# Column sets of the gated feed-forward units: one group later, with sums carried between PSUM banks by ScalarE copies

## What is computed

```python
def swiglu(x, w_gate, w_up, w_down):
    return (jax.nn.silu(x @ w_gate) * (x @ w_up)) @ w_down

for layer in range(DEPTH):            # first stack; the second has the same shape
    mix = even_mixer(hn, ...) if layer % 2 == 0 else odd_mixer(hn, ...)
    x = x + rms_norm(mix, norm_mix_post[layer])
    hn = rms_norm(x, norm_ffn_pre[layer])
    x = x + rms_norm(swiglu(hn, ...), norm_ffn_post[layer])

# in odd_mixer, per channel, the decay rate that a gate scales:
log_a = -RG_C * gate_r * jax.nn.softplus(-lam)
```

## Time and profile before

| what | value |
|---|---|
| median of 3 runs | 1228.73 us (1228.41 to 1228.79) |
| profiled execution | 1228.27 us, of which the span of its instructions 1226.4 us |
| TensorE (PE) busy | 1219.6 us, 99% |
| VectorE (DVE) busy | 1013.4 us, 83% |
| ScalarE (ACT) busy | 751.4 us, 61% |
| GpSimd (POOL) busy | 97.9 us, 8% |
| granted TensorE clock | 1.00 of full in the whole span |
| DMA, mean share of 16 engines | 4 to 6 tenths in most slices |

### The profile page before, as it was taken

One profiled execution on the slowest core, in us unless ns is written; L12 is line 12 of the kernel. 1 busy time (PEld: TensorE's weight loads), 2 busy tenths in 40 slices (PEclk: granted clock), 3 DMA queues, 4 the chain that ended last, 5 costly groups with the idle time before them and its releaser, 6 DMA issues.

```text
span 1226.4 us, 16404 instructions
## 1 busy us (share of the span) xinstructions
PE 1219.6 (99%) x6284; PEld 1013.5 (83%) x6284; DVE 1013.4 (83%) x1436; ACT 751.4 (61%) x1154; POOL 97.9 (8%) x123
## 2 busy tenths in 40 slices
PE   9999999999999999999999999999999999999998
PEld 7778888888888888888888888888888888888887
DVE  8986999889788798878887756988888785989787
ACT  8875756555998655555687536465556643745552
POOL 2520000000100100000232000000001300000000
PEclk9999999999999999999999999999999999999999
DMA  8544455546654564645555234556455315464552
GB/s 342 154 142 138 173 207 187 206 172 206 205 195 169 187 206 172 237 174 206 198 187 172 69 104 145 203 178 230 172 206 190 133 35 206 173 211 166 206 189 86
DMA packets 32830, 218.75 MB, mean 178 GB/s; under 512 B 3936, under 2 KB 4576, under 8 KB 7408
## 3 DMA queue, kind: packets, MB, share of 16 engines
q1 hardware_dynamic: 30384, 210.32, 48.8%
q0 software_dynamic: 1648, 6.88, 2.2%
q10 hardware_dynamic: 720, 0.50, 0.1%
HBM read 216.64 MB, written 1.05 MB: 177 GB/s over the span
## 4 chain that ended last, share of the span: by engine, by line
PE 94%; DVE 4%; issue 1%; ACT 1%; DMA 0%; SPq 0%; DVEq 0%; ACTq 0%
PE PS L521 26%; PE PS L523 26%; PE PS L522 26%; PE PS L527 6%; PE PS L1022 2%; PE PS L1046 1%; PE PS L558 1%; PE PS L630 1%; PE PS L624 1%; PE PS L625 1%; PE PS L556 1%; PE PS L555 1%; DVE WL L2050 1%; DMA RAW<-in_w 0%; PE PS L963 0%
## 5 line engine op out<-in xcount | busy, mean ns | idle before, releaser
L2050 DVE TENSOR_TENSOR WL<-RAW,WH 128x2048 fp32r<-128x2048 f32 (+3 forms) x198 | 420.8, 2131 | 97.8 <-ACT WH L1364 97.8
L1364 ACT ACTIVATE WH<-RAW 128x2048 fp32r<-128x2048 f32 (+3 forms) x200 | 356.6, 1789 | 119.2 <-PE PS L523 119.1
L521 PE MATMUL PS<-WH,HTh 128*128 128x512 f32 (+1 forms) x752 | 296.9, 395 | 0.1
L523 PE MATMUL PS<-WH,HTl 128*128 128x512 f32 (+1 forms) x752 | 291.6, 388 | 0.0
L522 PE MATMUL PS<-WL,HTh 128*128 128x512 f32 (+1 forms) x752 | 291.3, 387 | 0.0
L523 PEld LDWEIGHTS PS<-WH,HTl 128*128 128x128 f32 x752 | 141.2, 188 | 29.4
L521 PEld LDWEIGHTS PS<-WH,HTh 128*128 128x128 f32 x752 | 141.3, 188 | 29.3 <-DVE WL L2050 1.1
L522 PEld LDWEIGHTS PS<-WL,HTh 128*128 128x128 f32 x752 | 141.4, 188 | 26.9
L521 PE MATMUL PS<-WH,YAh 128*128 128x512 f32 x354 | 139.9, 395 | 0.1
L523 PE MATMUL PS<-WH,YAl 128*128 128x512 f32 x354 | 138.0, 390 | 0.0
L522 PE MATMUL PS<-WL,YAh 128*128 128x512 f32 x354 | 137.8, 389 | 0.0
(11 more groups left out here) (546 smaller groups left out, 2051.0 us busy)
## 6 DMA issues: line engine op xcount, KB each, us to landing
RAW<-in_w SPq DMA_DIRECT2D x196, 1024.0 KB, 4.9
WL<-in_w POOLq DMA_DIRECT2D x2, 1024.0 KB, 9.0
BC<-in_rows POOLq DMA_DIRECT2D x4, 512.0 KB, 4.1
YG<-in_mem POOLq DMA_DIRECT2D x4, 512.0 KB, 4.9
X<-in_x SPq DMA_DIRECT2D x2, 512.0 KB, 5.4
RAW<-in_w SPq DMA_DIRECT2D x4, 256.0 KB, 5.7
BC<-in_s SPq DMA_DIRECT2D x1, 512.0 KB, 11.3
YG<-in_s SPq DMA_DIRECT2D x1, 512.0 KB, 9.2
```

The lines of the kernel that those rows point to most:

```text
L521: e.matmul(out, ah, bh, start=start, stop=False, skip_group_check=joined)
L523: return e.matmul(out, al, bh, start=False, stop=stop, skip_group_check=joined)
L1364: e.activation(WH[:, c % NW, w], RAW[:, c % NR, w], ACT.Copy).then_inc(S.hi, 1)
L2050: e.tensor_tensor(WL[:, c % NW, w], RAW[:, c % NR, w], WH[:, c % NW, w].bitcast(f32), SUB).then_inc(S.lo, 1)
```

## The change

**Order of groups.** `SETS` becomes (3, 6), and each bank of a group and of a turned tile gets a new place (`BANKS`, `FOLD_BANK`). Turned tiles no longer have banks 4 and 5 for themselves.

**The set.** Of the four chunks of a set, the first two now carry 2 x 7 block products, and the last two are plain: again 90 matmuls. The sums stay in four banks in all, C11, C21, C12 and C22. After the first 6 matmuls ScalarE copies C11 to C22 (`cu`); after 12 it copies C12 into SBUF (`c7`); VectorE adds C22 and that copy into C21 (`j1`) after 24; ScalarE copies C22 to C12 (`cv`), and VectorE adds once more into C22 (`j2`). So two VectorE additions and three ScalarE copies stand where eight and one stood. TensorE waits for `cu`, `j1`, `cv` and `j2` within the set.

**Weight sums.** Per block row two sums are made ahead (`set_ahead`, `set_hi`) and two inside the set (`late_raw`, `late_hi`), rounded into the unused first quarter of `WH`/`WL` of the same chunk and two blocks of `YBh`/`YBl`. `RAW` of the two chunks is held until the late sums are made. The first plain chunk of the set is split in two halves of 2 x 512 (`half_of`, `half_rest`), the first of which has a semaphore of its own.

**Fold places.** Two tiles are turned at a time, between the two chunks of a group; groups 9 and 10 are turned inside `wide_mm`.

**Decay rates** move to the recurrent mixer, between its convolutions and splits.

```diff
-SETS = (2, 6)
+SETS = (3, 6)
+FOLD_BANK = (0, 6, 7, 0, 1, 6, 2, 3, 0, 6, 4)
 # TensorE
             def set_mm(f, a, cs, folds):
...
+                add(C11, Y(0, 0, 0), W(0, 1), start=True)
+                rests_ready(e, cs[1])
+                add(C11, Y(1, 0, 0), W(1, 1), stop=True).then_inc(S.qa, 1)
...
+                add(C12, sum_of(0, 2), T(0, 0, 1), start=True).then_inc(S.qt, 1)
+                add(C12, sum_of(1, 2), T(1, 0, 3), stop=True).then_inc(S.qt, 1)
+                e.wait_ge(S.cu, n + 1)
+                add(C22, sum_of(0, 1), T(0, 1, 2)).then_inc(S.qt, 1)
+                add(C22, sum_of(1, 1), T(1, 1, 4)).then_inc(S.qt, 1)
+                add(C11, Y(0, 1, 0), W(0, 2))
+                add(C11, Y(1, 1, 0), W(1, 2))
+                e.wait_ge(S.j1, n + 1)
+                add(C22, sum_of(0, 0), T(0, 0, 5))
+                add(C22, sum_of(1, 0), T(1, 0, 6)).then_inc(S.qc, 1)
+                e.wait_ge(S.n1l, n + 1)
+                for t, b in enumerate((C11, C21)):
+                    for k in (4, 5):
+                        rows(cs[2], k, t, 0, b)
+                e.wait_ge(S.cv, n + 1)
...
-                group(1)
-                fold(0)
-                set_mm(f, 2, cs[4:8], lambda: fold(1))
-                group(4)
-                fold(2)
-                fold(3)
-                group(5)
+                group(1)
+                group(2, lambda: two_folds(0))
+                set_mm(f, 3, cs[6:10], lambda: fold(2))
+                group(5, lambda: two_folds(3))
                 set_mm(f, 6, cs[12:16], lambda: fold(5))
-                group(8)
-                fold(6)
-                fold(7)
-                group(9)
-                fold(8)
+                group(8, lambda: two_folds(6))
+                group(9, lambda: fold(8))
                 group(10)
-                fold(9)
-                wide_mm(cs[22:], ..., lambda: fold(10), 1, f)
+                wide_mm(cs[22:], ..., lambda: two_folds(9), 1, f)
 # ScalarE
+                def column_set(a, *folds):
+                    half_of(cs[2 * a - 1], 0)
+                    e.wait_ge(S.qa, n + 1)
+                    copy(PS[:, C22, :], PS[:, C11, :]).then_inc(S.cu, 1)
+                    half_of(cs[2 * a - 1], 1)
+                    e.wait_ge(S.qt, 4 * n + 2)
+                    copy(FB[f][5][:, 3, :], PS[:, C12, :]).then_inc(S.c7, 1)
+                    late_hi(a, 0, 0)
+                    late_hi(a, 1, 0)
+                    tanh(a - 1)
+                    e.wait_ge(S.qc, n + 1)
+                    copy(PS[:, C12, :], PS[:, C22, :]).then_inc(S.cv, 1)
...
 # VectorE
+                def column_set(a, *folds):
+                    late_raw(a, 0, 0)
+                    late_raw(a, 0, 1)
+                    late_raw(a, 1, 0)
+                    half_rest(cs[2 * a - 1], 0)
+                    set_rest(a, 5, 0, 0)
+                    e.wait_ge(S.c7, n + 1)
+                    e.wait_ge(S.qt, 4 * n + 4)
+                    e.tensor_tensor(PS[:, C21, :], PS[:, C22, :], M7, ADD).then_inc(S.j1, 1)
...
+            decay_rates(2)
+            decay_rates(3)
             feed(PLAN["od0"][1])
             conv(0)
             mem_lo(0)
+            decay_rates(4)
             feed(PLAN["od1"][0])
             conv(1)
+            decay_rates(5)
             feed(PLAN["od1"][1])
             conv_lo(0)
             conv(2)
             conv(3)
+            decay_rates(6)
+            decay_rates(7)
             feed(PLAN["mem00"][0])
             conv_lo(1)
+            decay_rates(8)
```

More of the change, by code:

```diff
@@ L706, in fast_chunk, with set_mm @@
                 mul(2, Y(1, 1), T(3), False).then_inc(S.used, 1)
-            def early_chunk(f, a, first, c):
-                m, i = FASTS[c], 0 if first else 1
+            def set_mm(f, a, cs, folds):
+                n, m0 = set_n(f, a), 4 * FASTS[cs[0]]
+                C11, C21 = BANKS[a]
+                C12, C22 = BANKS[a + 1]
                 GSh, GSl = FB[f][8:10]
[L712 to L753, removed]
-                tk.then_inc(S.used, 1)
@@ L756, in set_mm, with W @@
[L756 to L770, removed]
-                folds()
-                early_chunk(f, a, True, cs[1])
-                plain(cs[2], 4)
-                early_chunk(f, a, False, cs[3])
+                def W(i, w):
+                    o, c = slice(512 * w, 512 * w + 512), cs[i]
+                    return WH[:, c % NW, o], WL[:, c % NW, o]
@@ new lines, in rows, with bank_free @@
+                def rows(c, k, t, half, b):
+                    o = (k % 2) * 1024 + half * 512
+                    return product(c, PS[:, b, :], (HTh, HTl), k, t, slice(o, o + 512), False, k == 7, True)
+                def bank_free(b):
+                    for g in in_bank(a, b):
+                        e.wait_ge(S.ylo, fold_n(f, g))
+                rests_ready(e, cs[0])
+                bank_free(C11)
+                add(C11, Y(0, 0, 0), W(0, 1), start=True)
+                rests_ready(e, cs[1])
@@ new lines, in set_mm @@
+                add(C21, Y(0, 1, 1), T(0, 1, 7))
+                add(C21, Y(1, 1, 1), T(1, 1, 8))
+                e.wait_ge(S.j2, n + 1)
+                rests_ready(e, cs[2])
+                for t, b in enumerate((C12, C22)):
+                    for k in (4, 5):
+                        tk = rows(cs[2], k, t, 1, b)
+                tk.then_inc(S.used, 1)
+                folds()
+                rests_ready(e, cs[3])
+                for t in range(2):
+                    for k in (6, 7):
+                        for half in range(2):
+                            tk = rows(cs[3], k, t, half, BANKS[a + half][t])
@@ L858, in group @@
+                def group(g, folds=None):
                     for n, c in enumerate(cs[2 * g:2 * g + 2]):
+                        if n and folds:
+                            folds()
                         rests_ready(e, c)
-                        for t in range(2):
+                        for t, b in enumerate(BANKS[g]):
                             if n == 0:
-                                free(g, t)
+                                free(g, b)
                             for k in range(4 * n, 4 * n + 4):
@@ L2176, in combine_second @@
                 join(E1, 7, V, 3)
-                if between:
-                    between()
                 join(PS[:, 3, :], 3, E1, 6)
```

346 lines of the change are left out of this document (212 added, 134 removed).

## The result

The changed kernel takes 1262.57 us (median of 4 runs, 1262.20 to 1262.64) against 1228.57 us (4 runs beside them): 1.0277 times as long, 95% interval 1.0259 to 1.0294. The forecast was 1259 in a range of 1244 to 1270. It is slower by 34.0 us where 30 to 31 were forecast.

The account below looks back on a forecast made before the run. TensorE was taken to bound the kernel, busy 1219.6 of 1226.4 us, its matmuls unchanged. New waits of 7.2 us in four units (28.9) plus 1.6 for decay rates gave 1258.8, said as 1259, range 1244 to 1270.

Parts of the forecast that it names:

- VectorE's relief: VectorE loses six additions per set, 29 us of work; worth nothing by itself, as TensorE did not wait.
- first set: First set of a unit: TensorE waits 0.16 us for a late sum's rest, 0.76 for C22, 0.64 for `j1`.
- second set, chunk's rest: Second set's second chunk: its rest ends a 25.3 us chain against 23.1 us of TensorE work, so 2.2 us late.
- second set, the others: Second set: 0.6 us for two sums and a rest behind the chunk's rest, 1.4 for C22 and `j1` again.
- fold 8: Rest of a unit: group 8's transposes wait for gates behind a VectorE rest, 0.25 us, between 0 and 0.5.
- group 9: End of a unit: group 9 is turned right ahead of the product that reads it, 1.2 us.
- decay rates, once: Mixer: 17 dependent operations delay the split of the convolution's second half, 1.6 us; 0 to 2.4 possible.
- the chain: VectorE and ScalarE work ahead of the second set, 25.3 us; rival that it does not form: 1248 us, chance 0.15.
- Loads were not late: Rival: loads or copies are slow because slots are freed later, loads adding 0 to 7 us; 1269 us, chance 0.08.
- The copies between banks: ScalarE's PSUM to PSUM copy: 0.60 us taken, at most 1.2; then 0 to 5 us more, `j1` returning most.
- The rate of matmuls: Rival: after the four 2.2 us waits some 14 matmuls each run slow, 12 us more; 1271 us, chance 0.05.
- TensorE's idle: Sign in the profile after: TensorE's idle rises from 6.8 to about 37 us.

Follow-up runs that it names:

- the narrow additions: Kernel before, with VectorE's eight additions per set 64 columns wide instead of 512, the other columns not added: 1228.35 us, ratio 0.9999.
- pauses: Kernel before, with TensorE made to wait for GpSimd additions eight times, two per unit: 1277.59 us with long pauses, 1249.90 us with short ones.
- the two edits that keep all of the work: Kernel after, with the decay rates back in the first unit and group 9 turned ahead of `wide_mm`: 1254.99 us, ratio 1.0218.

## Why the prediction was right

**Every wait named stands where it was put, and but for 0.4 us in the mixer they make the time.** VectorE's relief is worth nothing: the narrow additions gave 0.9999. The plain lists of what stands in each queue ahead of a signal gave all the rest.

| term, us a unit | forecast | measured (starts, unit 3 or the runs) |
|---|---|---|
| first set: late sum's rest, C22, `j1` | 0.16 + 0.76 + 0.64 = 1.56 | 0.14 + 0.57 + 0.56, and 0.11 behind each: 1.6 |
| second set, chunk's rest | 2.2 | 2.43 + 0.11 |
| second set, the others | 0.6 + 1.4 | 0.56 + 0.57 + 0.56, and 0.11 behind each: 2.0 |
| fold 8 (transposes of group 8) | 0.25 | 0.37 to 0.64 |
| group 9 | 1.2 | 1.2 to 1.4, restart included |
| unit | 7.2 | 8.0 |
| decay rates, once | 1.6 | 1.5 on `YAh`, restart included, and 0.4 on `ZN` |

**What was mis-sized.** The sum was 3.8 us short. The term missing in each wait is the restart: the step from the first matmul behind a wait to the second is 0.34 us, 0.11 over, some eight times a unit. The forecast took 0.23 for every matmul. It was in part made up for by too long a lateness for C22 (0.76 against 0.57; half of that is the restart behind the wait before, by which TensorE itself comes later). Such errors cancel in part, and that the total is this near is partly luck. Fold 8 was too small by 0.1 to 0.4, and the chain's slack by 0.2: the chain is right, 25.3 us, and TensorE's time beside it was a little less than the 23.1 reckoned. For the decay rates the wait on `YAh` came as forecast, and the one on `ZN` was missing: the forecast looked for one wait in the mixer only.

**The rivals.** The chain did form; without it the kernel takes 1251.5. Loads were not late: they land in 4.9 us, as before. The copies between banks were at the low end of the bounds, 0.58 us. Their place, not their length, counts, though the forecast was wrong that `j1` gives most of a longer copy back: it gave back 0.13 of 0.6. The rate of matmuls did fall behind the long waits, on 5 to 7 matmuls in three units, not 14 in four, and its 1 to 1.6 us fell into the next waits. That rival's mechanism is real, and its sum was wrong because it added the lower clock to waits that come anyway.

**TensorE's idle.** It was to rise to about 37 us; the page has 1260.7 - 1232.7 = 28.0. The slower matmuls and the longer first matmul behind a wait count as busy. Wait times in a table understate such a loss; distances of starts don't.

**Open.** Why about 2.43 us of waiting is followed by the lower clock in 18 cases of 28 and not in the others, and why some pauses bring 5 slow matmuls and others 11, no run here tells. With the copy made twice the same wait had it in the third unit as well (9 slow matmuls), with group 9 turned earlier in the first unit only. Whether a unit with the same scheme and other places for the turned tiles could do without the chain of 25 us wasn't tried; the two edits that keep all of the work leave it at 1254.99, slower than before.

## What to carry to other kernels

In a kernel whose TensorE hardly ever waits, work taken from another engine is worth nothing (28 us of it here), and a signal that is made late costs its full lateness: read each queue ahead of the signal and compare its sum with TensorE's. Where the queue behind a second wait does not depend on the first, the two waits are one debt, so taking away the first only lengthens the second (1262.85 for 1262.57). A long wait may be followed by half the clock, and whether that costs depends on what is late next: nothing in the kernel after, 1.5 to 2.9 us a time where all else was ready.

## What was not expected of the hardware

- A wait costs at least 0.11 us beyond itself: the second matmul behind it starts 0.34 us after the first, 0.23 in the flow, at the same clock. Behind the single pauses the steps that follow add 0.04 more.
- A wait of 2.43 to 2.45 us was enough for the lower clock 18 times of 28, and one of 2.79, but not 2.48, among the pauses; seven of 0.80 to 2.48 us had none. The slow stretch held 5 to 11 matmuls of 512 columns.
- ScalarE copies 128 x 512 from PSUM as fast to PSUM as to SBUF: 580 ns (16 copies) and 584 (3). The Trainium skill, "ScalarE: Activation LUTs", "What happens when an `exp` ACTIVATE runs", calls PSUM the faster place; these rows show no difference:

```profile
L1392 ACT ACTIVATE PS<-PS 128x512 f32<-128x512 f32 x16 | 9.3, 580 | 15.7 <-PE PS L531 15.7
L1392 ACT ACTIVATE ffn1TS<-PS 128x512 f32<-128x512 f32 x3 | 1.8, 584 | 2.1 <-PE PS L531 2.1
```
